# 512 ff columns at a time in the expert blocks, with the activation turned on VectorE

## The reference

```python
D_MODEL, SEQ, D_FF, N_EXPERTS, TOP_K = 1024, 256, 2752, 8, 2
def swiglu(x, w_gate, w_up, w_down):
    return (jax.nn.silu(x @ w_gate) * (x @ w_up)) @ w_down
def moe_ffn(x, w_router, w_gate, w_up, w_down):
    ...
    top_val, top_idx = lax.top_k(logits, TOP_K)
    top_w = jax.nn.softmax(top_val, axis=-1)
    ...        # token slots grouped by expert
    yp = lax.map(run, (xp.reshape(n_blocks, MOE_BLOCK, D), block_e)).reshape(P, D)
    contrib = yp[dest] * w_s[:, None].astype(x.dtype)
    out = jnp.zeros((T, D), x.dtype).at[tok_s].add(contrib)
```

## Time and profile before

| | us |
|---|---|
| median of 3 runs | 1289.18 |
| the profiled execution, its own time | 1291.01 |
| its span, first to last instruction | 1289.1 |
| TensorE busy | 1246.2 (97%) |
| VectorE busy | 592.2 (46%) |
| ScalarE busy | 411.7 (32%) |

### The profile page before, as it was taken

The page is one execution under the profiler, slowest core; times in us unless marked ns, Lnnn a source line. Parts: engine busy times, 40 slices in busy tenths (PEclk is TensorE's granted clock), DMA queues, the critical chain, the costliest instruction groups (busy, mean ns, idle before and its releaser), DMA issues.

```text
span 1289.1 us, 27080 instructions
## 1 busy us (share of the span) xinstructions
PE 1246.2 (97%) x11939; PEld 837.6 (65%) x11939; DVE 592.2 (46%) x1002; ACT 411.7 (32%) x735; POOL 44.0 (3%) x54
## 2 busy tenths in 40 slices
PE   6999999999999999999999999999999999999977
PEld 5787678888887887778755555555555555555533
DVE  6888987654444988988431212012122120211212
ACT  4444563634433544474311211111121111111100
POOL 0011010100000011010000000000000000000010
PEclk9999999999999999999999999999999999999999
DMA  9434434755534344436889999999999999999995
GB/s 345 160 133 162 150 125 153 257 193 196 184 133 149 131 164 146 181 133 254 372 320 400 419 399 389 415 417 419 417 418 419 379 393 422 416 419 417 420 420 237
DMA packets 58062, 376.29 MB, mean 292 GB/s; under 512 B 6322, under 2 KB 6914, under 8 KB 18004
## 3 DMA queue, kind: packets, MB, share of 16 engines
q1 hardware_dynamic: 56866, 370.17, 72.6%
q0 software_dynamic: 1072, 4.33, 1.0%
q10 hardware_dynamic: 2, 0.00, 0.0%
HBM read 371.07 MB, written 3.41 MB: 290 GB/s over the span
## 4 chain that ended last, share of the span: by engine, by line
PE 77%; DMA 7%; DVE 5%; SPq 1%; ACT 1%; issue 1%; POOL 0%; DVEq 0%; ACTq 0%
PE bank L2065 12%; PE bank L1680 8%; PE bank L1681 8%; PE bank L2084 8%; DMA ring<-in_moe 7%; PE bank L2074 6%; PE bank L1981 4%; PE bank L1730 4%; PE bank L2123 4%; PE bank L1958 3%; PE bank L2097 3%; PE bank L2103 3%; PE bank L2114 3%; PE bank L2148 2%; DVE ys L1144 1%; PE bank L2020 1%
## 5 line engine op out<-in xcount | busy, mean ns | idle before, releaser
L1155 DVE TENSOR_TENSOR w_lo<-raw,w_hi 128x2048 fp32r<-128x2048 f32 (+2 forms) x92 | 201.4, 2201 | 52.5 <-ACT w_hi L843 52.3
L1680 PE MATMUL bank<-w_hi,hT_hi 128*128 128x512 f32 (+1 forms) x528 | 209.3, 396 | 2.4 <-DVE hT_lo L1144 1.6
L1681 PE MATMUL bank<-w_hi,hT_lo 128*128 128x512 f32 (+1 forms) x528 | 205.1, 388 | 0.0
L843 ACT ACTIVATE w_hi<-raw 128x2048 fp32r<-128x2048 f32 (+2 forms) x92 | 169.1, 1847 | 88.7 <-PE bank L1730 42.7
L2065 PE MATMUL bank<-ring,hT_block 128*32 128x256 f32 (+1 forms) x2816 | 195.8, 374 | 0.0
L2084 PE MATMUL bank<-ring,hT_block 128*64 128x256 f32 (+1 forms) x1296 | 151.6, 378 | 6.5 <-DMA ring<-in_moe 6.3
L1561 DVE TENSOR_TENSOR both_k<-bank,odd_k 64x256 f32<-64x256 f32 (+1 forms) x44 | 18.1, 410 | 266.9 <-ACT odd_k L1077 266.9
L2065 PEld LDWEIGHTS bank<-ring,hT_block 128*32 128x32 f32 x2816 | 89.7, 110 | 68.6 <-issue 24.8
L1086 ACT ACTIVATE act_T<-bank 128x128 f32<-128x128 f32 (+1 forms) x88 | 26.8, 304 | 332.5 <-PE bank L2148 332.5
L2084 PEld LDWEIGHTS bank<-ring,hT_block 128*64 128x64 f32 x1296 | 88.8, 137 | 67.4 <-issue 17.9
L1565 DVE TENSOR_TENSOR act_moe<-silu_moe,bank 64x256 f32<-64x256 f32 (+1 forms) x88 | 36.7, 417 | 205.0 <-ACT silu_moe L1078 203.6
(11 more groups left out here) (286 smaller groups left out, 1502.3 us busy)
## 6 DMA issues: line engine op xcount, KB each, us to landing
ring<-in_moe SPq DMA_DIRECT2D x232, 1024.0 KB, 16.6
raw<-in_mix SPq DMA_DIRECT2D x56, 1024.0 KB, 4.8
raw<-in_dense SPq DMA_DIRECT2D x30, 1024.0 KB, 4.8
ring<-in_moe SPq DMA_DIRECT2D x16, 768.0 KB, 21.4
ring<-in_moe SPq DMA_DIRECT2D x8, 512.0 KB, 20.5
filters<-in_moe SPq DMA_DIRECT2D x2, 1024.0 KB, 10.1
gate_slots<-in_moe SPq DMA_DIRECT2D x2, 1024.0 KB, 10.8
ring<-in_moe SPq DMA_DIRECT2D x8, 256.0 KB, 18.2
```

Source lines behind the costliest of these rows:

```text
L843: nc.scalar.activation(HI[:, split_slot, 0:width], RAW[:, raw_slot, half:half + width], ACT.Copy)\
L1155: vec.tensor_tensor(LO[:, split_slot, 0:width], RAW[:, raw_slot, half:half + width], HI[:, split_slot, 0:width].bitcast(F32), ALU.subtract ...
L1680: mm(out_, left[0], right[0], start=start, stop=False)
L1681: mm(out_, left[1], right[1], start=False, stop=False)
```

## The change

Only the expert blocks change. The mixer and the dense FFN stay as they are.

- **Chunks.** `MOE_CHUNK` is 512: five full chunks and a last one of 192. A full chunk has four gate/up slabs and then, after the next chunk's gate/up slabs, two down slabs.
- **Light gate/up.** A moving operand holds one quarter's gate and up columns, twice: 512 moving columns in one matmul, two matmuls for each kd and 512 ff columns instead of four of 256.
- **Heavy gate/up.** For each kd three groups of 32 tokens, each with four matmuls of 256 moving columns on the four column tiles; each group has a bank of its own, and `odd_k` and `both_k` are gone. `x_banks(c)` takes banks 0 to 2 and 3 to 5 in turn, the outputs gather in banks 6 and 7.
- **Turning.** `turn_moe` on TensorE and the copy on ScalarE go. VectorE multiplies into `act_moe` and turns it in SBUF in 32 x 32 blocks: one instruction in a heavy chunk, eight small ones in a light one.
- **Tokens.** `hT_block` has room for two blocks. `pick_tokens` of the next block stands in chunk 3 (`PICK_AT`) instead of the last, and writes banks 0 and 1; ahead of chunk 4 TensorE waits until both have been copied out. Ahead of block 0 it now waits for both halves of the tokens before its first matmul.
- **Slabs.** All first slabs are full ones. The last down rows (64 of them) are padded to four groups of 32 in a tile of their own, `last_rows`, of which 16 rows in each group are loaded, with four DMAs of 16 partitions x 1024 floats (64 KB) in place of one of 256 KB; the other rows are zeroed once by GpSimd. A block has 33 places and `last_rows`.

```diff
+MOE_CHUNK = 2 * CHUNK
+QUARTER = P // 4
+MOE_SLABS = 34
+PICK_AT = 3
+MOE_WIDTHS = [SLAB] * 28 + [8 * TAIL] * 2 + [SLAB] * 2 + [D, D // 2]
...
-    tokens = region("tokens", KD * T, [[("hT_hi", [P, KD, T], F32R)], [("hT_block", [P, KD, CAP], F32)]])
+    tokens = region("tokens", KD * T, [[("hT_hi", [P, KD, T], F32R)], [("hT_block", [P, 2, KD, CAP], F32)]])
...
         def load_slab(e, b, at, p):
+            if p == MOE_SLABS - 1:
+                if at == 0:
+                    sp.wait_ge(sem("last_rows_zeroed"), 1)
+                else:
+                    sp.wait_ge(slab_used, MOE_SLABS * b + first)
+                rows = (TAIL - P) // 4
+                for q in range(4):
+                    sp.dma_start(R["last_rows"][QUARTER * q:QUARTER * q + rows, :],
...
-            for p in [0, 2, *range(4, FFN_SLABS)]:
-                if p == 18 and isinstance(b, int) and b:
+            for p in range(MOE_SLABS):
+                if p == 14 and isinstance(b, int) and b:
                     sp.wait_ge(y_taken, 2 * b)
...
+            def activate(b, c, n):
+                done_before = (MOE_CHUNKS + 1) * b + (Q_FIRST[1] + c)
+                act.wait_ge(act_done, done_before)
                 act.wait_ge(slab_used, n + 1)
+                nc.scalar.activation(per_group(R["silu_moe"], groups(b), c), x_parts(b, c)[0], ACT.Silu).then_inc(silu_done, 1)
...
+            def gate_times_up(b, c):
+                n = groups(b)
...
+                vec.tensor_tensor(per_group(act_tile(c), n, c), per_group(R["silu_moe"], n, c), x_parts(b, c)[1], ALU.mult).then_inc(act_done, 1)
+                dve.wait_ge(act_done, done_by)
+                tiles = 4 if c < MOE_CHUNKS else 2
+                if not is_heavy(b):
+                    for half in range(2):
+                        for t in range(2):
+                            for i in range(2):
+                                frm, to = QUARTER * (2 * half + t), QUARTER * (2 * half + i)
+                                ins = vec.transpose(R["act_T"][to:to + QUARTER, c % 2, 0:tiles, QUARTER * t:QUARTER * t + QUARTER],
+                                                    act_tile(c)[frm:frm + QUARTER, i * tiles * QUARTER:(i + 1) * tiles * QUARTER]
+                                                    .rearrange("p (j f) -> p j f", j=tiles))
+                    ins.then_inc(act_turned, 1)
+                    return
+                vec.transpose(R["act_T"][:, c % 2, 0:tiles, 0:n * QUARTER].rearrange("p j (t c) -> p t j c", t=n),
+                              act_tile(c)[:, 0:n * tiles * QUARTER].rearrange("p (t j f) -> p t j f", t=n, j=tiles)).then_inc(act_turned, 1)
...
+            def gate_up_moe(b, at, k0, nk, c):
+                width, tokens = 2 * quarter(c), tokens_of(b)
                 for k in range(nk):
                     kd = k0 + k
+                    if not is_heavy(b):
+                        for half in range(2):
+                            ins = mm(x_banks(c)[64 * half:64 * half + 64, 0, 0:2 * width], tokens[:, kd, 0:LCAP],
+                                     at[:, (4 * k + 2 * half) * width:(4 * k + 2 * half + 2) * width], start=kd == 0, stop=kd == KD - 1)
+                        continue
+                    for t in range(groups(b)):
+                        for q in range(4):
+                            ins = mm(x_banks(c)[QUARTER * q:QUARTER * q + QUARTER, t, 0:width], tokens[:, kd, QUARTER * t:QUARTER * t + QUARTER],
+                                     at[:, (4 * k + q) * width:(4 * k + q + 1) * width], start=kd == 0, stop=kd == KD - 1)
                 ins.then_inc(slab_used, 1)
...
+                for c in range(MOE_CHUNKS + 1):
+                    if c == PICK_AT + 1 and isinstance(b, int) and b < NE - 1:
+                        pe.wait_ge(front_ready, b + 2)
+                        pe.wait_ge(rear_ready, b + 2)
+                    slabs_of_c = gate_up_slabs(c)
+                    for i, p in enumerate(slabs_of_c):
+                        nk = KD // len(slabs_of_c)
+                        gate_up_moe(b, loaded(b, p, turns), i * nk, nk, c)
+                    if c == 0:
+                        continue
                     if c == 1 and isinstance(b, int) and b:
                         pe.wait_ge(y_taken, 2 * b)
+                    pe.wait_ge(act_turned, (MOE_CHUNKS + 1) * b + c)
+                    if c == PICK_AT and isinstance(b, int) and b < NE - 1:
                         pick_tokens(b + 1, ROOM[b + 1])
+                    down_chunk(c - 1)
```

More of the change, by code:

```diff
@@ L140, in moe_place, with gate_up_slabs, down_slabs, quarter @@
 def moe_place(b, p):
-    return FFN_PLACES * b + ffn_place(p, is_late(b, p))
-def slab_of(place, late):
-    return 2 * place + 1 if place < 2 else place if late and place >= LATE_SLAB else place + 2
+    return MOE_PLACES * b + p + (SKIPPED if is_late(b, p) else 0)
+def gate_up_slabs(c):
+    first = 0 if c == 0 else 6 * c - 2
+    return range(first, first + (4 if c < MOE_CHUNKS else 2))
+def down_slabs(c):
+    first = gate_up_slabs(c + 1)[-1] + 1 if c < MOE_CHUNKS else MOE_SLABS - 2
+    return range(first, first + 2)
+def quarter(c):
+    return (MOE_CHUNK if c < MOE_CHUNKS else TAIL) // 4
 def place_before(place):
@@ L159, in freed_by @@
     if b < NE:
[L160 to L163, removed]
+        before, slab = divmod(place_before(place), MOE_PLACES)
+        return before - b, slab
+    place -= MOE_PLACES * b + (2 * RING if p in REJOINED else RING)
+    return (-1, place + MOE_PLACES) if place < 0 else (0, place if place < LATE_SLAB else place - SKIPPED)
 CHUNKS = ["v", "x1", "q", "x2", "k", "av", "g0", "g1", "g2", "g3"]
@@ L704, in slot_free @@
                 blocks, slab = freed_by(at, p)
-                sp.wait_ge(slab_used, FFN_SLABS * b + (FFN_SLABS * blocks + slab + 1 + first))
+                sp.wait_ge(slab_used, MOE_SLABS * b + (MOE_SLABS * blocks + slab + 1 + first))
             elif slot == "h":
@@ L2107, in heavy_down @@
                 first_two(0)
-                ins = last_third(0, stop and not whole)
-                if whole:
-                    last_third(1, stop)
-                    for half in range(2):
-                        for t in range(2):
-                            q = 64 * half + 32 * t
-                            ins = mm(PS[4 + half][q:q + 32, :], R["act_T"][:, parity, 1, 32 * t:32 * t + 32], part(1, half),
-                                     start=False, stop=False)
-                ins.then_inc(slab_used, 1)
@@ L2152, in moe_block @@
[L2152 to L2165 removed]
+                ins = last_third(0)
@@ new lines, in moe_block, with down_chunk @@
+            def moe_block(b, turns=None, amid=None):
+                down = heavy_down if is_heavy(b) else light_down
+                def down_chunk(c):
+                    for i, p in enumerate(down_slabs(c)):
+                        at = loaded(b, p, turns)
+                        down(R["act_T"][:, c % 2, 2 * i:2 * i + 2, :], (at[:, 0:D], at[:, D:2 * D]), c == 0 and i == 0, False, 1)
+                if not isinstance(b, int) or b == 0:
+                    pe.wait_ge(front_ready, b + 1)
+                    pe.wait_ge(rear_ready, b + 1)
+                for c in range(MOE_CHUNKS + 1):
+                    if c == PICK_AT + 1 and isinstance(b, int) and b < NE - 1:
[7 more added lines that the diff above has]
+                        continue
@@ L2172, in moe_block @@
-                turn_moe(b, NCH, rows)
+                    down_chunk(c - 1)
                 if amid:
                     amid()
-                pe.wait_ge(act_copied, (NCH + 1) * b + (NCH + 1))
-                last_at = loaded(b, 35, turns)
-                down(loaded(b, 34, turns), 0, False, True, False)
-                (heavy_down_last if heavy else light_down_last)(last_at)
+                pe.wait_ge(act_turned, (MOE_CHUNKS + 1) * b + (MOE_CHUNKS + 1))
+                at = loaded(b, MOE_SLABS - 2, turns)
@@ L2180, in turn_spread @@
+                pe.wait_ge(last_rows_loaded, 64 * b + 64)
+                down(R["act_T"][:, MOE_CHUNKS % 2, 0:2, :], (at, R["last_rows"]), False, True, 2)
             def turn_spread(b):
```

268 lines of the change are left out of this document (113 added, 155 removed).

## The result

| | us, median |
|---|---|
| before | 1288.49 (6 runs, 1287.99 to 1290.49) |
| changed | 1294.56 (6 runs, 1292.22 to 1297.05) |
| ratio | 1.0045, 95% interval 1.0031 to 1.0059 |

The forecast was 1278.7 with a range of 1273 to 1286. The time lies outside, on the other side, next to what rival 1 gave: 1295.1.

What follows compares the result with a forecast made beforehand. The expert stage was taken to be bound by a 270.5 MB stream at about 418.5 GB/s: 1291.0 - 3.0 - 4.0 - 4.6 - 0.9 + 2.0 = 1280.5 us profiled, 1.8 above the median, so 1278.7; range 1273 to 1286.

Steps and rivals of the forecast that it cites:

- rival 1: End of each block's loads: small pieces hold up the stream, 2.3 us a block, 18.4 in all; 1295.1 us; chance 0.10.
- the term for `last_rows`: Four 64 KB pieces into 16 partitions each, every block: 0.25 us a block, 2.0 lost in all, ends 0 and 18.4.
- the dips from 760 and from 1010: Two 50 us stretches at 383 and 380 GB/s while TensorE is full: 4.0 and 4.6 us come back.
- the price of 1.71 us for gate/up: Light blocks: with 512 columns a gate/up slab costs TensorE the same as a down slab, 1.71 us, instead of 1.83.
- The first load into a freed slot: SP's queue, waiting for the fifth place's use: stays at about 647, as before at 647.14; 0 us gained.
- VectorE's eight turns: Light chunk: 0.26 us each within a chain of some 3 us, hidden from TensorE; waits beyond 2 us would be absent.
- From 650: 50 us stretch in a light block at 377 GB/s: 3.0 of 5.0 lost us come back, ends 0 and 5.0.
- the picking: Chunk 3: copying the next block's tokens costs 0 us; gate/up of chunk 4 waits behind with slabs in store.
- The end of the block: Last block, from the last 1 MB slab to its last matmul: 3.8 us instead of 4.8; 0.9 less, ends -1.0 and 1.2.
- Rival 2: Stream's dips are the memory's doing, not TensorE's, so only the end changes: 1290.3 us, no change; chance 0.11.
- Rival 3: Eight expert blocks: all of TensorE's 40 us is gained, 1249 us; chance 0.02.
- Rival 4: Light blocks: TensorE's clock falls in the new waits for slabs; two such blocks give 1334.7 us, slower; chance 0.02.

Runs made afterwards that it cites:

- run 2: Changed kernel with last_rows loaded by one DMA of 128 partitions x 512 floats, same 256 KB, data in wrong rows: 1280.31 us, ratio 0.9925.
- run 4: Changed kernel with last_rows loaded by four DMAs of 128 partitions x 128 floats, 64 KB each, data in wrong rows: 1281.87 us, ratio 0.9944.
- run 10: Changed kernel with last_rows loaded whole with its zeros, one DMA of 128 partitions x 1024 floats, 512 KB: 1285.32 us, ratio 0.9969.
- run 12: Kernel of Run 9 with light gate/up matmuls of 256 moving columns again in place of 512: 1281.64 us, ratio 0.9945.
- runs 1: Changed kernel without the load of last_rows, 2.1 MB less in the stream: 1276.43 us, ratio 0.9897.
- Run 9: Changed kernel with last_rows folded into one DMA of 128 partitions x 512 floats, VectorE turning three tiles in the last chunk, result correct: 1280.02 us, ratio 0.9931.

## Why the prediction was wrong

**The step that failed is the term for `last_rows`.** It stood at 2.0 us for eight blocks (0.25 each) between ends of 0 and 18.4; it measures 14.2 (run 2 against the changed kernel), 1.8 us a block, far up in the bounds and past the point of 1.6 from which the change is slower. I had taken the value near "nothing" because the nearest row, a store from 96 partitions, leaves no dip in the stream. That was the wrong row: a store reads SBUF, it takes 96 partitions and not 16, and no run tried its shape as a load. It was also read loosely. The store that the prediction means goes out at 1210.17, and the stretch that it cites begins at 1230; the rate from 1210 to 1230 is 421 GB/s, so the statement holds for that store, but not by that row. The fixed time of a lone 256 KB transfer, 2.3 us, which I used as the upper end, came out close, but by chance: run 4 has four transfers in place of one and pays 0.2 us a block.

The gain that stood against this term was too high as well: on the medians run 2 is 8.9 us faster than before, not 12.5. Of the 3.6 us, 1.5 are the scale (the profiled execution of before lay 1.8 us above its median, that of run 2 lies 0.3 above), and most of the rest is under the small errors below. 14.2 lost and 8.9 gained make 5.3, and with the shift of some 0.8 between the measurements the 6.1 us that the change lost.

**What held.** The reading that the stage is a stream at 418.5 GB/s, and that TensorE's gain is worth what the stream had lost, holds: in run 2 the dips from 760 and from 1010 are gone (predicted 4.0 and 4.6 back of 4.2 and 4.6), TensorE waits 31.6 us for slabs while the stream runs at 419 to 420 GB/s, and in run 10 more bytes cost exactly their time at that rate. TensorE's own prices held too, though the price of 1.71 us for gate/up was put down to the 512 columns, which run 12 shows to be worth 0.01 us of it: the 1.83 us that it was compared with the earlier trace rows is a slab with a turn behind it. In the changed kernel a light slab of gate/up costs 1.72 us (from 638.07 to 644.96 it uses four) and a heavy chunk 15.5:

```profile
638.07 1.94 PE L2121 MATMUL bank<-h_slot,hT_block 128*64 128x512 f32 x8 [1.01 <-ACT hT_block L1133]
644.96 3.63 PE L2121 MATMUL bank<-ring,hT_block 128*64 128x512 f32 x16
722.86 10.54 PE L2126 MATMUL bank<-ring,hT_block 128*32 128x256 f32 x192
738.37 10.54 PE L2126 MATMUL bank<-ring,hT_block 128*32 128x256 f32 x192
```

The first load into a freed slot goes out at 646.91, beside 647.14. VectorE's eight turns take 0.30 us each and the heavy one 0.58 (form, busy, mean ns, idle before), and TensorE waits for none of them:

```profile
L1623 DVE STREAM_TRANSPOSE act_T<-act_moe 32x128 f32<-32x128 f32 x160 | 48.4, 303 | 2.6
L1628 DVE STREAM_TRANSPOSE act_T<-act_moe 128x384 f32<-128x384 f32 x20 | 11.6, 579 | 0.7
```

**Small errors.** Without the pieces the forecast's sum was 1291.0 - 12.5 = 1278.5 on the profile's scale; run 2's profiled execution takes 1280.6. From 650 the stream got 50 x (392-377)/418.5 = 1.8 us back instead of 3.0. Run 2's stretches say where (the changed kernel's three are 348, 420 and 346 GB/s):

```profile
650.00:660.00 10.00, 10.00 (x50) 4.04 (x48) 8.85 (x44) 0.38 (x1) 0.00 (x0) 1.00 0.99 389
660.00:680.00 20.00, 20.00 (x210) 9.10 (x208) 10.05 (x48) 1.80 (x6) 0.00 (x0) 1.00 0.99 401
680.00:690.00 10.00, 10.00 (x50) 3.38 (x48) 2.61 (x9) 0.38 (x1) 0.00 (x0) 1.00 0.95 341
```

From 650 to 680 run 2 has more than the kernel before (364 and 375 GB/s in the same two stretches), but from 680 to 690 nothing came back (346 before). In the changed kernel this stands behind the longest wait of SP there (670 to 690 us), and run 2 has the same wait of 6.0 us:

```profile
SPq L795 <- PE bank L2157: 8.5, 3, 6.0
```

It waits 6.0 us for the first down slab of chunk 2 to be used: picking, 2.8 us, stands ahead of that slab, and so do the slots that do not come back. I had counted the picking as free because TensorE had slabs in store; SP had no slot in store. No run tested this dip by itself, so its cause is argued, not shown.

The end of the block, after the last 1 MB slab: 0.9 less was forecast. In run 2 it lasts from 1265.20 to 1268.32 + 1.03, 4.15 us against 4.8, 0.6 less.

**The rivals.** Rival 1 happened, within a microsecond of its time, though not by its mechanism (a lone landing for each block). That its 1295.1 came so close is luck: its 18.4 lost against 12.5 gained are both too high, by about as much as each other. Its counter-argument, that neighbours overlap, is what failed: the slabs beside the pieces are themselves slowed. At 0.10 it had too little: the change made a shape of load that the trace showed nowhere, in the very resource that I had just named as the bound. Rival 2 is refuted by run 2: the dips go, so the memory had no reason of its own for them. (The change both gives slots sooner and makes the first slabs of a block full ones; no run tells which of the two filled the first microseconds of the dips.) Rival 3 is refuted by run 2 as well (1280 us where it gave 1249, with the stream at 419 to 420). Rival 4 showed once, below, for a few us and not for blocks.

**The Trainium skill's rule.** It stood beside rival 1. The Trainium skill (SBUF — State Buffer, Door 1: The DMA port swizzle) says that a DMA's rate depends on the ports that its partitions reach, and the estimate from its map was 1.9 us a block for four transfers on four ports each. Measured: 1.8. But ports counted for each transfer do not sort the other runs. 64 neighbours and 16 partitions at a stride of eight reach eight ports by the map and should be cheaper; they cost 2.1 us a block each. Counted over a whole set, the changed kernel's four pieces reach eight ports too, as these two do, and all three cost about the same; but then the two halves reach all 16 between them, and still cost 1.4. The direction agrees and the size for one case agrees, but neither count gives all the runs. The Trainium skill, DMA: Bandwidth & Descriptors, The descriptor swizzle, says that in a transfer over 128 partitions each engine writes one port that no other of them writes. That would fit all the runs (any transfer with fewer partitions makes engines meet at a port), but no run here shows which engine wrote what, and this stays open.

## What to carry to other kernels

When a stream of loads is the bound, look first at the shape of every load that a change adds, not at its bytes: in a saturated stream 256 KB over all 128 partitions cost 0.5 us (runs 1 and 2), over 64 partitions 2.6. Pad or fold a short load until it takes all partitions, even at twice the bytes (runs 9 and 10). And a unit cost that is on the bound and stands in no row deserves the middle of its range and a chance to match, not the end at which the nearest row of another kind lies.

## What the runs showed of the hardware that was not expected

- **The shape of a load in a full stream.** Above the one wide transfer of 256 KB, a block: four of 16 partitions 1.8 us (neighbours) and 2.1 (stride 8), one of 64 partitions 2.1, two of 64 partitions 1.4, four of 128 partitions 0.2. The DMA share stays at 1.01 to 1.02 meanwhile, so the share does not show it; the GB/s do, and the packets' times. Slow packets alone do not name the cause: in the old dip of the kernel before, where SP waits for slots, the 8 KB packets are slow as well (340 ns from 775 to 800), with a share of 0.99 over the 50 us.
- **The stream's end.** It frays earlier in the changed kernel and in runs 2 and 9. Before, the rate stays at 416 GB/s until the last 8 us and then falls:

```profile
1264.00:1268.00 4.00, 3.83 (x40) 2.17 (x36) 0.00 (x0) 0.28 (x1) 0.00 (x0) 1.00 1.01 416
1268.00:1272.00 4.00, 3.37 (x28) 1.65 (x26) 1.71 (x2) 0.38 (x1) 0.00 (x0) 1.00 0.81 331
1272.00:1276.00 4.00, 2.96 (x32) 1.91 (x32) 0.50 (x2) 0.60 (x2) 0.00 (x0) 1.00 0.33 133
```

  In the changed kernel the share sinks over 16 us:

```profile
1264.00:1268.00 4.00, 2.81 (x14) 0.49 (x8) 0.05 (x1) 0.39 (x1) 0.00 (x0) 1.00 0.94 358
1268.00:1272.00 4.00, 3.02 (x14) 1.06 (x16) 3.84 (x10) 0.00 (x0) 0.00 (x0) 1.00 0.68 275
1272.00:1276.00 4.00, 3.81 (x36) 2.12 (x32) 1.52 (x2) 0.00 (x0) 0.00 (x0) 1.00 0.50 208
1276.00:1280.00 4.00, 1.99 (x10) 0.57 (x8) 2.14 (x9) 0.25 (x1) 0.00 (x0) 1.00 0.24 87
```

  Run 9, without narrow loads, has it too (0.70, 0.53 and 0.44 in the 12 us from 1254). A narrow load is therefore not the cause. That some of the 16 engines are done long before others would explain it, but no row here tells the engines apart, so it is not shown.
- **The clock fell once in the stage.** In the changed kernel's block 2 a wait for a slab left TensorE nearly idle, and the granted clock went to 0.50, the level of 1.2 GHz, until it had worked again:

```profile
848.00:850.00 2.00, 0.19 (x2) 0.00 (x0) 0.00 (x0) 0.00 (x0) 0.00 (x0) 1.00 1.08 338
850.00:852.00 2.00, 1.57 (x6) 0.63 (x8) 0.00 (x0) 0.00 (x0) 0.00 (x0) 0.71 0.98 277
852.00:854.00 2.00, 2.00 (x8) 0.38 (x6) 0.00 (x0) 0.00 (x0) 0.00 (x0) 0.50 0.97 397
```

  It stands behind a block's narrow loads, in a wait of 2.2 us. Narrow loads are not needed for it: run 2 has such a fall too, in a heavy block, behind 2.8 us in which TensorE did nothing and waited for nothing that the profile shows:

```profile
1180.00:1182.00 2.00, 0.00 (x0) 0.00 (x0) 0.00 (x0) 0.00 (x0) 0.00 (x0) 0.88 1.00 410
1182.00:1184.00 2.00, 1.73 (x32) 1.47 (x36) 0.00 (x0) 0.13 (x1) 0.00 (x0) 0.50 1.01 422
```
